# Index scores of a sparse-attention decoder step: cached keys as the moving operand, two units side by side

## Chip, cores and metric

One core of a Trainium2 chip runs the whole program. The metric is the device time of one execution, in microseconds (us); lower is better.

## The reference, cut to what matters

A two-layer decoder trunk is run once for a prompt of 1024 tokens and for 8 sample sequences of 8 tokens, each with 4096 cached positions. Layer 0 is sparse attention: an "indexer" with 4 heads of 64 dimensions scores every key for every query, and the 256 best are attended to. The change touches the index scores alone.

```python
# prompt: 1024 new tokens; sample: 8 sequences x 8 new tokens, each with 4096 cached positions
IDX_HEADS = 4
IDX_DIM = 64
IDX_SCALE = (IDX_DIM ** -0.5) * (IDX_HEADS ** -0.5)
...
def dsa_block(q, qi, wi, q_pos, k_all, v_all, ki_all, topk):
    L = k_all.shape[1]
    key_pos = jnp.arange(L, dtype=jnp.int32)
    logits = jnp.einsum('bqhd,bsd->bqhs', qi.astype(jnp.float32), ki_all.astype(jnp.float32))
    score = jnp.einsum('bqh,bqhs->bqs', wi.astype(jnp.float32), jax.nn.relu(logits)) * IDX_SCALE
    admissible = key_pos[None, :] <= q_pos[:, None]
    score = jnp.where(admissible[None], score, -jnp.inf)
    _, sel = lax.top_k(score, topk)
...
```

## The kernel before, in words

The program is a row of stages, each a block in which the engines run their own instruction lists and meet at a barrier at its end. `index_stage` computes the index projections; `score_stage` (lines 2848 to 3109) computes all index scores; `search_stage` begins after it and searches the 256th best score. TensorE (PE) is in order, and so is each other engine.

In `score_stage` two kinds of work share the engines.

**Units.** The cached index keys of the sample sequences are handled in 32 units: sequence b of 8 and quarter c of 4, each 1024 keys by 64 dimensions, held as 128 partitions by 512 values. GpSimd gathers them in groups of four (`IndexUnits.gather`, L2699, four indirect DMAs), with room for two groups: the gather of group k waits until unit 4k-5 has been turned (`turned`). `turn` (L2972) transposes a unit by four 128x128 transposes, ScalarE copies it to `kxT` (`key_copy`, L3026), and then four products of 64 columns (L3005) have the keys as the weights and the queries of the sequence (`q_pair`) as the moving operand. Each product is two fp32 passes, so a unit has eight weight loads of 128 columns. VectorE takes ReLU and the head weight in one instruction (`weigh`, L3086), and adds up the heads (`sum_heads`, L3094). The scores then lie with the keys on the partitions; `back` (L2981) transposes them once more, twice in a quarter, eight times in all, and ScalarE copies them with a stride to `Ss` (`back_copy`, L3034). The head weights reach all partitions by a product with ones (L2992).

**Works.** 44 `logit` works compute the new tokens' scores: s0 to s3 (64 columns) are the samples' new keys, then come four heads of each piece of the prompt's rows 2 to 7 (L2960, L2961; up to 512 columns). ScalarE takes ReLU (L3020), VectorE weighs and adds (L3075, L3078). The logits have two banks, so `logit(s)` waits for the ReLU of work s-2. Each of the units 0 to 11 has two works, each of the others one.

The stage's order on PE is: turn of unit i+1, works of unit i, products of unit i. GpSimd's list also holds the causal masks: two selects on the samples' new scores after work s3 (L2933, L2936) ahead of the gather of group 2, and one select for each prompt row block (L2946), placed by `masks_after` between the gathers; the one for row 2 waits for work s7 and stands ahead of gather 3, that for row 4 waits for s19 and stands ahead of gather 5.

Some products elsewhere in the program use a part of the array's columns: `sample_attention_stage` multiplies by weights of 32 columns, four products with four outputs of 32 partitions side by side, and keys of 512 columns as the moving operand (L3968).

Of the kernel before, what the change touches and what calls it, by code (L numbers as in the profile page):

```python
# [2847 lines left out]
def score_stage(nc, idx, wi_row, kidx_outs, units, room, Ss, Sp, prompt_level, g):  # L2848
# [7 lines left out]
    with Scope(nc, "sel") as S:  # L2856
        fresh = room.take(NS)[0:NS, :]
        by_key = room.take(NT * NB * NQ).rearrange("p (t b q) -> p t b q", t=NT, b=NB)
        ki_nat = room.take(NTT * ID).rearrange("p (n d) -> p n d", n=NTT)
        kxT = room.take(2 * 512).rearrange("p (s x) -> p s x", s=2)  # L2860
# [4 lines left out]
        weighed = room.low(TOK, 2 * UK * NQ * IH).rearrange("p (s t x) -> p s t x", s=2, t=UK)  # L2865
        w_all = room.low(TOK + 512, NS * IH).rearrange("p (b q h) -> p b q h", b=NB, q=NQ)
        w_row = room.low(TOK + 768, NS * IH)[0:IH, :].rearrange("p (b q h) -> p b q h", b=NB, q=NQ)
# [19 lines left out]
        backs_of = {i: [i // 8 * 2 - 2 + i % 8 - 2] if i >= 8 and i % 8 in (2, 3) else [] for i in range(len(units_))}  # L2887
        last_backs = range(2 * UNITS - 2, 2 * UNITS)
        turns = [("unit", 0)]
        for i in range(len(units_)):  # L2890
            if i + 1 < len(units_):
                turns.append(("unit", i + 1))
            turns += [("back", n) for n in backs_of[i]]
        turns += [("back", n) for n in last_backs]
        turn_no = {x: e for e, x in enumerate(turns)}
        assert len(turns) == len(units_) + NT // 4
# [4 lines left out]
        wb, small = S.ps("wb", [P, 512]), S.ps("small", [P, 512])  # L2901
        nat_of = lambda n: small[:, (n + 1) * ID:(n + 2) * ID] if n < 7 else wb[:, NS * IH + (n - 7) * ID:NS * IH + (n - 6) * ID]
        products, relu_ready, summed, masked = (S.sem(n) for n in ("products", "relu_ready", "summed", "masked"))
        q_zero, q_ready, w_row_ready, wb_ready, w_ready = (S.sem(n) for n in
                                                           ("q_zero", "q_ready", "w_row_ready", "wb_ready", "w_ready"))
        turned, kxT_ready, part_ready, part_used, by_key_ready = (S.sem(n) for n in ("turned", "kxT_ready", "part_ready",
                                                                                    "part_used", "by_key_ready"))
        back_turned, back_copied, begun = S.sem("back_turned"), S.sem("back_copied"), S.sem("begun")
# [4 lines left out]
        def wait_copied(eng, e):  # L2913

            kind, n = turns[e]
            eng.wait_ge(kxT_ready if kind == "unit" else back_copied, n + 1)

        @block.sync
        def _(sp):
            for n in range(NTT):  # L2920
                sp.wait_ge(i_copied, n + 1)
                sp.dma_start(i_p[n * P:n * P + rows(n), :] if n < NTT - 1 else i_s, ki_nat[0:rows(n), n, :]).then_inc(i_stored, 16)
            sp.wait_ge(i_stored, 16 * NTT)

        @block.gpsimd
        def _(pool):
            nc.gpsimd.memset(q_pair[:, :, :, :, :], 0.0).then_inc(q_zero, 1)
            nc.gpsimd.memset(Ss[0:NS, PAST // 2:], LOWEST).then_inc(begun, 1)
            nc.gpsimd.memset(prompt_level[:, :], 0.0)

# [19 lines left out]
        def _(pe):  # L2950
# [13 lines left out]
            def turn(i):  # L2964
                k, j = i // AHEAD, i % AHEAD
                if j == 0:
                    units.wait_loaded(pe, k)
                e = turn_no["unit", i]
                if e >= 2:
                    wait_copied(pe, e - 2)  # L2970
                for t in range(4):
                    last = nc.tensor.transpose(tr[e % 2][:, t * P:(t + 1) * P], kx[:, k % 2, j, t * P:(t + 1) * P],  # L2972
                                               g["ident"][:, :])
                last.then_inc(turned, 1)

            def back(n):
                e = turn_no["back", n]
                wait_copied(pe, e - 2)
                pe.wait_ge(by_key_ready, NB * (n // 2 + 1))
                for t in range(4):  # L2980
                    last = nc.tensor.transpose(tr[e % 2][0:NS, t * P:(t + 1) * P],  # L2981
                                               by_key[:, 4 * n + t, :, :].rearrange("p b q -> p (b q)"), g["ident"][:, :])
                last.then_inc(back_turned, 1)
# [10 lines left out]
            for i, (b, c) in enumerate(units_):  # L2994
                if i + 1 < len(units_):
                    turn(i + 1)
                for s in works_of[i]:
                    logit(s)
                if i == 0:
                    pe.wait_ge(q_ready, 2 * IH)  # L3000
                pe.wait_ge(kxT_ready, i + 1)
                if i >= 2:
                    pe.wait_ge(part_used, i - 1)
                for t in range(4):
# [3 lines left out]
                for n in backs_of[i]:  # L3008
                    back(n)
            for n in last_backs:  # L3010
                back(n)

        @block.scalar
        def _(act):
# [7 lines left out]
            def key_copy(i):  # L3022
                act.wait_ge(turned, i + 1)
                if i >= 2:
                    act.wait_ge(part_ready, i - 1)
                nc.scalar.activation(kxT[:, i % 2, :], tr[turn_no["unit", i] % 2][:, :], ACT.Copy).then_inc(kxT_ready, 1)  # L3026

            def back_copy(n):
                act.wait_ge(back_turned, n + 1)
                c, t0 = n // 2, 4 * (n % 2)  # L3030
                half, c = c // 2, c % 2

                dst = Ss[64 * half:64 * half + NS, c * 1024:(c + 1) * 1024].rearrange("q (p t) -> q t p", t=UK)
                nc.scalar.activation(dst[:, t0:t0 + 4, :],  # L3034
                                     tr[turn_no["back", n] % 2][0:NS, :].rearrange("q (t p) -> q t p", t=4),
                                     ACT.Copy).then_inc(back_copied, 1)

            key_copy(0)
            act.wait_ge(wb_ready, 1)
            nc.scalar.activation(w_all[:, :, :, :].rearrange("p b q h -> p (b q h)"), wb[:, 0:NS * IH], ACT.Copy,  # L3040
                                 scale=IDX_SCALE).then_inc(w_ready, 1)
            for i in range(len(units_)):
# [3 lines left out]
                if i + 1 < len(units_):  # L3046
                    key_copy(i + 1)
                for s in works_of[i]:
                    relus(s)
                for n in backs_of[i]:  # L3050
                    back_copy(n)
            for n in last_backs:
                back_copy(n)

        @block.vector
        def _(dve):
            for h in range(IH):
                nc.vector.tensor_scalar(w_row[:, :, :, h], wi_row[:, SEQ:TOK].rearrange("p (b q) -> p b q", b=NB),
                                        g["ident"][0:IH, h:h + 1], None, ALU.mult).then_inc(w_row_ready, 1)
# [21 lines left out]
            def weigh(i):  # L3081
                b, c = units_[i]
                dve.wait_ge(part_ready, i + 1)
                if i >= 2:
                    dve.wait_ge(by_key_ready, i - 1)
                nc.vector.scalar_tensor_tensor(  # L3086
                    out=weighed[:, i % 2, :, :], in0=part[i % 2][:, 0:UK * NQ * IH].rearrange("p (t x) -> p t x", t=UK),
                    scalar=0.0, in1=w_all[:, b, :, :].rearrange("p q h -> p (q h)").unsqueeze(1).to_broadcast([P, UK, NQ * IH]),
                    op0=ALU.max, op1=ALU.mult).then_inc(part_used, 1)

            def sum_heads(i):
                b, c = units_[i]
                dve.wait_ge(part_used, i + 1)
                nc.vector.tensor_reduce(out=by_key[:, UK * c:UK * (c + 1), b, :],  # L3094
                                        in_=weighed[:, i % 2, :, :].rearrange("p t (q h) -> p t q h", h=IH),
                                        axis=AX.X, op=ALU.add).then_inc(by_key_ready, 1)

            dve.wait_ge(wi_ready, 2)
            for i in range(len(units_)):
                for s in works_of[i]:  # L3100
                    add_head(s)
                if i == 0:
                    dve.wait_ge(w_ready, 1)
                if i < NTT:
                    nc.vector.tensor_copy(ki_nat[0:rows(i), i, :], nat_of(i)[0:rows(i), :]).then_inc(i_copied, 1)
                weigh(i)
# [1224 lines left out]
```

## Time and profile before

| | us |
|---|---|
| median of the 3 runs (2519.26 to 2523.59) | 2520.27 |
| profiled execution, its own time | 2533.14 |
| its span, first to last instruction | 2531.4 |
| PE busy over the span | 2444.0 (97%) |
| `score_stage`, first PE instruction to the last copy | 71.0 to 149.7 |

An engine that is busy for the whole span is not always the bound of each stage; the granted clock of PE (1.00 is 2.4 GHz, 0.50 is 1.2 GHz) changes what the same instructions take.

### The profile page before, as it was taken

Reading aid. Unit: us, or ns where it says so; the run is one execution under the profiler, and the core shown is the slowest. Engines: PE = TensorE matmul, PEld = TensorE weight load, DVE = VectorE, ACT = ScalarE, POOL = GpSimd, SP = SyncE. Lnnn points to the kernel's source line nnn. Section 1 sums busy time; section 2 is a strip of 40 time slices with the busy share of each in tenths; the row PEclk is TensorE's granted clock in tenths of the full one; section 3 lists DMA queues with packets and bytes.
Section 4 is the critical chain, followed back from the end, with each engine's and each line's share of the span. In section 5 each row is a group of like instructions: output and inputs, shape, how many; then the busy total and the mean of one; then the engine's idle time right before and its main releaser. Section 6 shows DMA issues by size and latency. Waiting matters only on the chain. (4 is left out here: it accounts for less than half of the span.)

```text
span 2531.4 us, 49311 instructions
## 1 busy us (share of the span) xinstructions
PE 2444.0 (97%) x18922; PEld 2332.5 (92%) x18953; DVE 1827.9 (72%) x3377; ACT 1130.0 (45%) x1928; POOL 108.3 (4%) x140
## 2 busy tenths in 40 slices
PE   8999898899999999999999999989999999999998
PEld 7899865577899999999999999989999999999998
DVE  6668867777558888886685686764798888768642
ACT  5567677686534433333222353553443434322221
POOL 1310132200000000000000000000000000000000
PEclk9899999999999999999999999999999999999999
DMA  6312499820022343433694423234143434449522
GB/s 213 88 51 80 145 332 361 329 84 1 21 100 70 139 147 138 147 138 124 241 321 150 134 73 113 68 94 168 56 139 138 148 138 151 140 177 351 193 91 84
DMA packets 279016, 371.91 MB, mean 147 GB/s; under 512 B 20747, under 2 KB 219651, under 8 KB 270662
## 3 DMA queue, kind: packets, MB, share of 16 engines
q1 hardware_dynamic: 266998, 294.23, 34.3%
q0 software_dynamic: 11776, 75.50, 8.1%
q8 instruction: 101, 1.65, 0.3%
q14 instruction: 61, 0.50, 0.1%
q10 hardware_dynamic: 80, 0.02, 0.0%
HBM read 271.07 MB, written 98.63 MB: 146 GB/s over the span
## 5 line engine op out<-in xcount | busy, mean ns | idle before, releaser
L1554 PE MATMUL ffn_acc<-trunk_x_ahead,trunk_w_hi 128*128 128x272 f32 x2464 | 466.5, 289 | 2.7 <-PEq L87 2.7
L1554 PE MATMUL ffn_acc<-ffn_x_later,ffn_w_hi_more 128*128 128x272 f32 x2112 | 397.1, 287 | 1.5 <-DVE trunk_xT L1203 1.4
L1554 PEld LDWEIGHTS ffn_acc<-trunk_x_ahead,trunk_w_hi 128*128 128x128 f32 x2464 | 385.3, 188 | 3.3 <-issue 3.3
L1554 PE MATMUL ffn_acc<-trunk_x_ahead,trunk_w_lo 128*128 128x272 f32 x1232 | 352.9, 286 | 0.0
L1554 PEld LDWEIGHTS ffn_acc<-ffn_x_later,ffn_w_hi_more 128*128 128x128 f32 x2112 | 330.9, 188 | 2.3 <-issue 2.3
L1554 PE MATMUL ffn_acc<-ffn_x_later,ffn_w_lo_more 128*128 128x272 f32 x1056 | 304.1, 288 | 0.0
L1554 PEld LDWEIGHTS ffn_acc<-trunk_x_ahead,trunk_w_lo 128*128 128x128 f32 x1232 | 232.5, 189 | 0.0
L1554 PEld LDWEIGHTS ffn_acc<-ffn_x_later,ffn_w_lo_more 128*128 128x128 f32 x1056 | 198.8, 188 | 0.0
L1445 DVE TENSOR_TENSOR trunk_xT<-ffn_acc,trunk_xT 128x544 f32<-128x544 f32 x168 | 121.4, 723 | 92.9 <-PE ffn_acc L1610 91.0
L1610 PE MATMUL ffn_acc<-trunk_x_ahead,trunk_w_hi 128*128 128x272 f32 x896 | 170.8, 289 | 0.0
L945 ACT ACTIVATE ffn_w_hi_more<-trunk_w_raw 128x512 fp32r<-128x512 f32 x132 | 83.3, 631 | 156.2 <-PE ffn_acc L1554 153.5
L945 ACT ACTIVATE trunk_w_hi<-ffn_w_sum 128x512 fp32r<-128x512 f32 x88 | 55.6, 632 | 210.2 <-DVE ffn_w_sum L1184 125.4
L1610 PE MATMUL ffn_acc<-ffn_x_later,ffn_w_hi_more 128*128 128x272 f32 x768 | 145.8, 287 | 0.1
L1634 PE MATMUL ffn_acc<-trunk_x_ahead,trunk_w_hi 128*128 128x364 f32 (+1 forms) x576 | 142.1, 328 | 0.0
L1610 PEld LDWEIGHTS ffn_acc<-trunk_x_ahead,trunk_w_hi 128*128 128x128 f32 x896 | 140.1, 188 | 0.4 <-issue 0.4
L1610 PE MATMUL ffn_acc<-trunk_x_ahead,trunk_w_lo 128*128 128x272 f32 x448 | 128.3, 286 | 0.0
L3321 PE MATMUL search_acc<-attxm_x_pairs,attxm_w_hi 128*128 128x364 f32 (+1 forms) x480 | 121.4, 334 | 1.9 <-PEq L87 1.9
L1610 PEld LDWEIGHTS ffn_acc<-ffn_x_later,ffn_w_hi_more 128*128 128x128 f32 x768 | 120.2, 188 | 0.7 <-issue 0.3
L1032 ACT ACTIVATE trunk_xT<-trunk_xT 128x544 fp32r<-128x544 f32 x112 | 71.7, 654 | 91.5 <-DVE trunk_xT L1264 48.8
L1610 PE MATMUL ffn_acc<-ffn_x_later,ffn_w_lo_more 128*128 128x272 f32 x384 | 110.5, 288 | 0.0
L1203 DVE TENSOR_TENSOR trunk_xT<-ffn_acc,ffn_u 128x544 f32<-128x544 f32 x88 | 63.5, 722 | 59.2 <-PE ffn_acc L1554 59.2
L1634 PEld LDWEIGHTS ffn_acc<-trunk_x_ahead,trunk_w_hi 128*128 128x128 f32 x576 | 101.8, 188 | 0.0
(523 smaller groups left out, 5994.6 us busy)
## 6 DMA issues: line engine op xcount, KB each, us to landing
o_kept<-trunk_xT SPq DMA_DIRECT2D x96, 544.0 KB, 4.4
trunk_w_raw<-in_ffn_w_gu SPq DMA_DIRECT2D x88, 512.0 KB, 4.0
trunk_x_ahead<-o_kept SPq DMA_DIRECT2D x56, 544.0 KB, 6.7
ffn_x_later<-o_kept SPq DMA_DIRECT2D x56, 544.0 KB, 7.3
x_saved<-trunk_xT SPq DMA_DIRECT2D x24, 544.0 KB, 2.7
trunk_xT<-x_saved SPq DMA_DIRECT2D x24, 544.0 KB, 6.6
o_kept<-trunk_xT SPq DMA_DIRECT2D x32, 272.0 KB, 4.9
trunk_w_raw<-in_sg_w_in SPq DMA_DIRECT2D x16, 512.0 KB, 4.0
```

Source lines behind the costliest of these rows:

```text
L945: nc.scalar.activation(w_parts(i)[0], source, ACT.Copy).then_inc(w_hi_ready, 1)
L1032: nc.scalar.activation(stage_hi[STAGE_OF[i][0]], raw_block[i], ACT.Copy).then_inc(kept_hi, 1)
L1203: nc.vector.tensor_tensor(two(out), pair(b), two(a), ALU.add).then_inc(done, 1)
L1445: nc.vector.tensor_tensor(two(out), pair(bank_of(z, n)), two(out), ALU.add).then_inc(d_added, 1)
L1554: last = nc.tensor.matmul(bank(2 * PAIR[p] + c)[:, 0:QC], w[:, k * P:(k + 1) * P], x(p, k)[:, c * QC:(c + 1) * QC], start=FRESH[p] and k = ...
L1610: last = nc.tensor.matmul(bank(2 * bank_of(z, n) + c)[:, 0:QC], w[:, k * P:(k + 1) * P], x(i, at)[:, c * QC:(c + 1) * QC], start=n in (0, ...
L1634: last = nc.tensor.matmul(bank(NC3 * (q % 2) + c)[:, 0:w], part[:, q % 2, k * P:(k + 1) * P], x[:, a:a + w], start=(k == 0 and j == 0), st ...
L3321: last = nc.tensor.matmul(banks[NC3 * (m % 2) + c][:, 0:w], part[:, k * P:(k + 1) * P], x_parts[x][:, k, a:a + w], start=(k == 0 and j == ...
```

## The change

The queries of a sequence (64 columns) are now the weights, and a unit's 512 transposed key columns are the moving operand. Two units are scored side by side: the even one has its output in partitions 0 to 63 of a bank, the odd one in 64 to 127. VectorE takes ReLU alone, over both units in one instruction (`gate`). The head weights and the scale stand in a masked matrix `w_sum`, built by nine GpSimd instructions and four on VectorE from weights that go through a small DRAM tensor; once in eight units (four pairs) eight products with weights of 32 columns (`sum_heads`) give the scores with the queries on the partitions. `back` and the product with ones are gone. VectorE (`left_out`) and ScalarE (`right_out`) copy the result to `Ss`, two strided copies each. Turns run two units ahead, with four buffers of `kxT` in place of two. The twelve extra works are spread over all 32 units: s3 is now in unit 2, s7 in unit 5, s11 in unit 8, s19 in unit 14. The order in which the keys' rows are stored is changed to 7, 8, 0 to 6. Gathers and masks keep their places and waits.

```diff
-        by_key = room.take(NT * NB * NQ).rearrange("p (t b q) -> p t b q", t=NT, b=NB)
-        kxT = room.take(2 * 512).rearrange("p (s x) -> p s x", s=2)
+        kxT = room.take(4 * 512).rearrange("p (s x) -> p s x", s=4)
+        first, second = room.low(TOK, 2 * 512), room.take(2 * 512)
+        gated = [v[:, 512 * i:512 * (i + 1)] for v in (first, second) for i in range(2)]
+        w_sum = room.take(4 * 2 * 4 * NQ).rearrange("p (m s b q) -> p m s b q", m=4, s=2, b=4)
+        w_cols = room.take(4)
...
-            n = 1 + (i < n_extra)
+            n = 1 + ((i + 1) * n_extra // len(units_) - i * n_extra // len(units_))
...
+            sp.dma_start(w_kept.rearrange("q h b -> h b q"), wi_row[:, SEQ:TOK].rearrange("h (b q) -> h b q", b=NB)
+                         ).then_inc(w_stored, 16)
+            sp.wait_ge(w_stored, 16)
+            for u in range(2):
+                for s in range(2):
+                    at = 64 * u + 32 * s
+                    sp.dma_start(w_cols[at:at + 32, :], w_kept.rearrange("q h (m u) -> u (q h) m", u=2)[u]).then_inc(w_loaded, 16)
...
+            nc.gpsimd.memset(w_sum[:, :, :, :, :], IDX_SCALE).then_inc(w_masked, 1)
+            pool.wait_ge(w_masked, 1)
+            for m in range(4):
+                v = w_sum[:, m, :, :, :]
+                nc.gpsimd.affine_select(out=v, in_=v, compare_op=ALU.is_ge, fill=0.0, base=128 * (m % 2),
+                                        pattern=[[-32, 2], [-64, 4], [-4, NQ]], channel_multiplier=1).then_inc(w_masked, 1)
...
+            def sum_heads(c):
+                pe.wait_ge(gated_ready, 4 * c + 4)
+                if c:
+                    pe.wait_ge(left_copied, 2 * c)
+                    pe.wait_ge(right_copied, 2 * c)
+                else:
+                    pe.wait_ge(w_ready, 4)
+                    pe.wait_ge(i_copied, NTT)
+                for odd in range(2):
+                    for quad in range(2):
+                        m = 2 * quad + odd
+                        for s in range(2):
+                            at = 64 * quad + 32 * s
+                            last = nc.tensor.matmul(sums_bank[quad][at:at + 32, :],
+                                                    w_sum[:, m, s, :, :].rearrange("p b q -> p (b q)"), gated[m],
+                                                    start=odd == 0, stop=odd == 1, skip_group_check=True)
+                last.then_inc(heads_summed, 1)
...
-            pe.wait_ge(w_row_ready, IH)
-            nc.tensor.matmul(wb[:, 0:NS * IH], g["ones"][0:IH, :], w_row[:, :, :, :].rearrange("p b q h -> p (b q h)"),
-                             start=True, stop=True).then_inc(wb_ready, 1)
...
-                for t in range(4):
-                    last = nc.tensor.matmul(part[i % 2][:, t * 64:(t + 1) * 64], kxT[:, i % 2, t * P:(t + 1) * P],
-                                            q_pair[:, b, :, :, :].rearrange("p s q h -> p (s q h)"), start=True, stop=True)
+            turn(1)
+            for j in range(n_pairs):
+                for i in (2 * j, 2 * j + 1):
+                    if i + 2 < len(units_):
+                        turn(i + 2)
+                    for s in works_of[i]:
+                        logit(s)
+                if j == 0:
+                    pe.wait_ge(q_ready, 2 * IH)
+                pe.wait_ge(kxT_ready, 2 * j + 2)
+                if j >= 2:
+                    pe.wait_ge(gated_ready, j - 1)
+                for u in range(2):
+                    i = 2 * j + u
+                    b, c = units_[i]
+                    last = nc.tensor.matmul(part[j % 2][64 * u:64 * (u + 1), :],
+                                            q_pair[:, b, :, :, :].rearrange("p s q h -> p (s q h)"), kxT[:, i % 4, :],
+                                            start=True, stop=True, skip_group_check=True)
                 last.then_inc(part_ready, 1)
+                if j and j % 4 == 0:
+                    sum_heads(j // 4 - 1)
+            sum_heads(n_pairs // 4 - 1)
...
+            def right_out(c):
+                act.wait_ge(heads_summed, c + 1)
+                for s in range(2):
+                    dst, src = sums_out(c, 1, s)
+                    nc.scalar.activation(dst, src, ACT.Copy).then_inc(right_copied, 1)
...
+            def gate(j):
+                dve.wait_ge(part_ready, j + 1)
+                if j >= 4:
+                    dve.wait_ge(heads_summed, j // 4)
+                nc.vector.tensor_scalar(gated[j % 4], part[j % 2][:, :], 0.0, None, ALU.max).then_inc(gated_ready, 1)
+
+            def left_out(c):
+                dve.wait_ge(heads_summed, c + 1)
+                for s in range(2):
+                    dst, src = sums_out(c, 0, s)
+                    nc.vector.tensor_copy(dst, src).then_inc(left_copied, 1)
```

## Rows read from the trace of the kernel before

**Rows 1.** The page: busy time, share of the span and instructions of each engine.
```profile
PE 2444.0 (97%) x18922; PEld 2332.5 (92%) x18953; DVE 1827.9 (72%) x3377; ACT 1130.0 (45%) x1928; POOL 108.3 (4%) x140
```
**Rows 2.** Stretches: length, then busy time of the five engines, clock, DMA share, GB/s.
```profile
71.00:149.70 78.70, 72.70 (x524) 68.05 (x524) 50.28 (x131) 45.58 (x86) 27.11 (x35) 0.89 0.31 85
71.20:84.85 13.65, 13.65 (x69) 12.49 (x67) 5.50 (x25) 4.42 (x11) 2.52 (x7) 0.50 0.03 7
84.85:125.80 40.95, 38.30 (x305) 35.90 (x305) 29.59 (x73) 26.71 (x52) 19.89 (x23) 1.00 0.50 134
122.40:125.80 3.40, 1.78 (x15) 1.68 (x15) 1.51 (x5) 2.80 (x5) 0.30 (x1) 1.00 0.31 93
125.80:129.20 3.40, 3.40 (x18) 3.40 (x18) 2.03 (x6) 1.09 (x2) 1.75 (x2) 0.50 0.14 19
```
**Rows 3.** Timeline of PE, three units: start, duration, engine, line, operation.
```profile
85.26 0.61 PE L2972 MATMUL sel_banks<-trunk_ident,att_proj 128*128 128x128 f32 x4
87.25 0.28 PE L2972 MATMUL sel_banks<-trunk_ident,att_proj 128*128 128x128 f32 x1
...
92.04 0.61 PE L2972 MATMUL sel_banks<-trunk_ident,att_proj 128*128 128x128 f32 x4
...
94.27 0.28 PE L2972 MATMUL sel_banks<-trunk_ident,att_proj 128*128 128x128 f32 x1
...
140.32 0.61 PE L2972 MATMUL sel_banks<-trunk_ident,att_proj 128*128 128x128 f32 x4
...
141.23 1.00 PE L3005 MATMUL sel_banks<-att_proj 128*128 128x64 f32 x8
142.07 0.28 PE L2972 MATMUL sel_banks<-trunk_ident,att_proj 128*128 128x128 f32 x1
```
**Rows 4.** Products with 32-column weights in the later stage: by line, then the timeline of PE.
```profile
L3968 PE MATMUL satt_sc<-satt_KT,satt_qs x256: 589/593/618, 320.7 to 474.0; 128*32 128x512 f32 x128
...
397.54 1.09 PE L3954 MATMUL satt_tr<-trunk_ident,cache_ring 128*128 128x128 f32 x8
398.78 1.07 PE L3968 MATMUL satt_sc<-satt_KT,satt_qs 128*32 128x512 f32 x8
399.77 0.33 PE L3954 MATMUL satt_tr<-trunk_ident,att_proj 128*128 128x128 f32 x1
```
**Rows 5.** Start of the stage, timeline of PE.
```profile
73.03 1.12 PE L2972 MATMUL sel_banks<-trunk_ident,att_proj 128*128 128x128 f32 x4
74.08 1.22 PE L2992 MATMUL sel_wb<-att_proj,trunk_ones 4*128 4x256 f32 x2
```
**Rows 6.** GpSimd ahead of gather 2, and stretches of 1 us around its landing.
```profile
81.36 0.28 POOL L2933 TENSOR_SCALAR_AFFINE_SELECT att_proj<-att_proj 64x64 f32<-64x64 f32 x1 [8.38 <-DVE att_proj L3078]
...
83.22 0.95 POOL L2699 DMA_INDIRECT att_proj<-in_cache_kidx,trunk_unit_row  x1 [1.16 <-PE sel_banks L2972]
...
90.00:91.00 1.00, 0.92 (x5) 0.62 (x5) 0.77 (x2) 1.00 (x4) 0.00 (x0) 1.00 0.16 45
91.00:92.00 1.00, 1.00 (x10) 0.96 (x9) 1.00 (x4) 1.00 (x3) 0.00 (x0) 1.00 0.00 0
```
**Rows 7.** Stalls inside the stage, of PE and of ScalarE.
```profile
108.19 0.66 PE L2972 MATMUL sel_banks<-trunk_ident,att_proj 128*128 128x128 f32 x4 [0.92 <-ACT scores_Ss L3034]
...
122.99 1.08 ACT L3034 ACTIVATE scores_Ss<-sel_banks 64x512 f32<-64x512 f32 x1 [2.20 <-remote]
...
124.12 0.66 PE L2972 MATMUL sel_banks<-trunk_ident,att_proj 128*128 128x128 f32 x4 [1.62 <-ACT scores_Ss L3034]
```
**Rows 8.** The end of the stage, timeline.
```profile
144.34 1.00 PE L3005 MATMUL sel_banks<-att_proj 128*128 128x64 f32 x8
...
147.06 1.03 PE L2981 MATMUL sel_banks<-trunk_ident,att_proj 128*64 128x128 f32 x8 [1.71 <-DVE att_proj L3094]
147.69 1.99 ACT L3034 ACTIVATE scores_Ss<-sel_banks 64x512 f32<-64x512 f32 x2 [2.55 <-PE sel_banks L2981]
```
**Rows 9.** Groups of VectorE by line and shape: busy us, mean ns, idle before.
```profile
L3086 DVE SCALAR_TENSOR_TENSOR att_proj<-sel_banks,att_proj 128x256 f32<-128x256 f32 x32 | 13.4, 418 | 3.8 <-PE sel_banks L3005 2.2 <-remote 1.6
...
L4147 DVE COPY satt_probT<-satt_tr 128x512 f32<-128x512 f32 x24 | 16.5, 686 | 5.0 <-PE satt_tr L4002 3.4 <-remote 1.3
```

More of the change, by code:

```diff
@@ L2885, in score_stage @@
         assert at_work == len(work) and 0 <= n_extra <= len(units_)
[L2887 to L2896, printed above, removed]
+        n_pairs = len(units_) // 2
+        keys_order = (7, 8) + tuple(range(7))
         banks = S.ps("banks", [P, 6 * 512])
@@ L2911, in score_stage, with sums_out @@
         block = S.block()
-        def wait_copied(eng, e):
-            kind, n = turns[e]
-            eng.wait_ge(kxT_ready if kind == "unit" else back_copied, n + 1)
+        def sums_out(c, quad, s):
+            rows, half = 64 * (c // 2) + 32 * quad, c % 2
+            dst = Ss[rows:rows + 32, half * 1024:(half + 1) * 1024].rearrange("q (p t s) -> q s t p", t=4, s=2)[:, s, :, :]
+            at = 64 * quad + 32 * s
+            return dst, sums_bank[quad][at:at + 32, :].rearrange("q (t p) -> q t p", t=4)
         @block.sync
         def _(sp):
-            for n in range(NTT):
-                sp.wait_ge(i_copied, n + 1)
+            sp.dma_start(w_kept.rearrange("q h b -> h b q"), wi_row[:, SEQ:TOK].rearrange("h (b q) -> h b q", b=NB)
[5 more added lines that the diff above has]
+                    sp.dma_start(w_cols[at:at + 32, :], w_kept.rearrange("q h (m u) -> u (q h) m", u=2)[u]).then_inc(w_loaded, 16)
+            for k, n in enumerate(keys_order):
+                sp.wait_ge(i_copied, k + 1)
                 sp.dma_start(i_p[n * P:n * P + rows(n), :] if n < NTT - 1 else i_s, ki_nat[0:rows(n), n, :]).then_inc(i_stored, 16)
@@ L2929, in _ @@
             nc.gpsimd.memset(prompt_level[:, :], 0.0)
+            nc.gpsimd.memset(w_sum[:, :, :, :, :], IDX_SCALE).then_inc(w_masked, 1)
[4 more added lines that the diff above has]
+                                        pattern=[[-32, 2], [-64, 4], [-4, NQ]], channel_multiplier=1).then_inc(w_masked, 1)
+            pool.wait_ge(w_masked, 5)
+            for m in range(4):
+                v = w_sum[:, m, :, :, :]
+                nc.gpsimd.affine_select(out=v, in_=v, compare_op=ALU.is_ge, fill=0.0, base=IH - 1 - 128 * (m % 2),
+                                        pattern=[[32, 2], [64, 4], [4, NQ]], channel_multiplier=-1).then_inc(w_masked, 1)
             pool.wait_ge(summed, IH)
@@ L3045, in _ @@
                     nc.scalar.activation(Ss[NS:P, PAST // 2:], fresh, ACT.Copy)
-                if i + 1 < len(units_):
-                    key_copy(i + 1)
+                if i + 2 < len(units_):
+                    key_copy(i + 2)
                 for s in works_of[i]:
                     relus(s)
[L3050 to L3053, printed above, removed]
+                if i > 8 and i % 8 == 2:
+                    right_out(i // 8 - 1)
+            right_out(UNITS - 1)
         @block.vector
         def _(dve):
-            for h in range(IH):
-                nc.vector.tensor_scalar(w_row[:, :, :, h], wi_row[:, SEQ:TOK].rearrange("p (b q) -> p b q", b=NB),
-                                        g["ident"][0:IH, h:h + 1], None, ALU.mult).then_inc(w_row_ready, 1)
             dve.wait_ge(nat_turned, NTT)
@@ L3101, in _ @@
                     add_head(s)
-                if i == 0:
-                    dve.wait_ge(w_ready, 1)
                 if i < NTT:
-                    nc.vector.tensor_copy(ki_nat[0:rows(i), i, :], nat_of(i)[0:rows(i), :]).then_inc(i_copied, 1)
-                weigh(i)
-                if i:
-                    sum_heads(i - 1)
-            sum_heads(len(units_) - 1)
+                    n = keys_order[i]
+                    nc.vector.tensor_copy(ki_nat[0:rows(n), n, :], nat_of(n)[0:rows(n), :]).then_inc(i_copied, 1)
+                if i == 4:
+                    dve.wait_ge(w_loaded, 16 * 4)
+                    dve.wait_ge(w_masked, 9)
+                    for m in range(4):
+                        nc.vector.tensor_scalar(w_sum[:, m, :, :, :], w_sum[:, m, :, :, :], w_cols[:, m:m + 1], None,
+                                                ALU.mult).then_inc(w_ready, 1)
+                if i % 2:
+                    gate(i // 2)
+                if i > 8 and i % 8 == 2:
+                    left_out(i // 8 - 1)
+            left_out(UNITS - 1)
 PIECE = TOK // 8
```

85 lines of the change are left out of this document (19 added, 66 removed).

## The prediction

> **What bounds the kernel now.** I read the page first: PE is busy for 97% of the span [rows 1], so PE's own list sets the time, stage by stage. The change lives in one stage, 71.0 to 149.7. Its stretches say that PE is busy for 72.7 of 78.7 us there, VectorE 50.3, ScalarE 45.6, and that the clock is not whole: it is 0.50 from 71.2 to 84.85 and again from 125.8 to 129.2 [rows 2]. So PE bounds this stage, and everything saved on PE counts once, unless PE then waits for something that is now hidden.
>
> The timeline of PE gives the cost of each piece. A unit with one 512-column work takes 142.07 - 140.32 = 1.75 us, one with two takes 94.27 - 92.04 = 2.23, one with two 384-column works 87.25 - 85.26 = 1.99 [rows 3]. So a 512-column work is 0.48, a 384-column one (1.99 - 1.27) / 2 = 0.36, and an empty unit 1.27. The products with the queries are 142.07 - 141.23 = 0.84 of that [rows 3] (0.83 below, so that the parts add up), the four transposes the other 0.44. Works narrower than 384 I take at 0.24, the nearest bound below being half of the 512's. All 44 works: 24 x 0.48 + 8 x 0.36 + 12 x 0.24 = 17.3 us. Before, at full clock, PE has 32 x 0.44 + 32 x 0.83 + 17.3 + 8 backs x 0.44 + 0.6 (half of the 1.2 that L2992 took at half clock [rows 5]) = 62.1 us. From 73.03 [rows 5] to 149.7 are 76.7. The other 14.6: the half clock gives away (84.85 - 73.03) / 2 = 5.9 and 1.7; PE's two stalls 1.6 and 0.9 [rows 7]; 3.4 at the end, where PE's list is dry but for a microsecond [rows 8]; 1.1 unassigned.
>
> **Scoring.** 32 x 0.83 = 26.6 goes. In its place are 16 pairs of two 64-column products with 512 moving columns, two fp32 passes each. The trace has no 64-column tile. Nearest are the 32-column ones: eight passes (four products) begin at 398.78 and the next PE work at 399.77, 0.99 us, while a single pass lasts 0.59 [rows 4]. Two rounds of four passes, 1.07 - 0.59 = 0.48 apart, fit; eight in a row don't. And 0.48 is what one pass costs alone: L2992, two passes of 256 columns at half clock, took 1.22 [rows 5], so some 0.5 for 512 at full. Between the transposes (eight by 0.11 from 397.54, over at 398.4) and 398.78 lie one bf16 product of 512 columns and a gap: about 0.1 for coming into this mode. So a pair costs 0.99 + 0.1 = 1.1, all of it on the path: 17.6 in all. Bounds: 0.95 (no gap) and, if two 64-column tiles don't overlap, 2.0.
>
> The Trainium skill bears on the gap (TensorEngine Tiling (Array Packing), Key Properties): changing the tiling mode drains the engine, and by its Restrictions fp32 transposes can't run in a column-tiled mode, so every pair pays twice. The rows agree with a small price. It also has a measured packing (TensorE: Matmul & The Clock Gate, Measured speedup vs the span model): three column tiles gave 2.38 times, not 3. By that ratio a pair would be some 0.2 dearer, 3 us in all, an estimate; the rows show four tiles at the cost of one.
>
> **Head sums.** Added: 4 x (8 products, 16 passes, four rounds). By the same rows 4 x 0.48 + 0.1 = 2.0, so 8.0. Removed: eight backs, 3.5, and L2992, 0.6 (1.2 as it ran). Bounds: 1.8, or 7 each if nothing overlaps.
>
> **PE's list after:** 14.1 + 17.3 + 17.6 + 8.0 = 57.0 against 62.1: 5.1 us less.
>
> **Other engines.** VectorE loses 32 x (0.42 + 0.41) and gets 16 gates; a copy of 128x512 from PSUM takes 0.69 [rows 9]; so it falls by 15 us, less 8 strided copies of 0.7 to 1.1 and four small scalings. ScalarE has eight strided copies as before (1.0 to 1.1 each [rows 8]). Per pair ScalarE then has some 4.75 instructions of 0.5 and a quarter of 2.2, 2.9 us, against PE's 3.6; it doesn't become the bound. SyncE's round trip through DRAM (5 small DMAs, ahead of the key rows) has over 10 us until VectorE wants `w_cols` in unit 4; GpSimd's nine new instructions of 0.3 lie in the idle 8.4 us ahead of 81.36 [rows 6]. Both cost nothing; without the cover, 2 to 3 us. The spread of the works moves no PE time by itself.
>
> **What comes late next: gathers.** The gather of group 2 stands behind the selects that wait for s3. At half clock PE does turns 0 to 2, s0, turn 3, s1, pair 0 (about 2.0) and turn 4 by 80.3, s2 and s3 by 81.15; before, s3's last pass began at 79.94 and the selects at 81.36 [rows 6]. So the selects start near 82.4 and the gather near 83.2, as before (83.22). Its traffic ended in the slice 90 to 91 [rows 6]: landed near 90.3, 7.1 us after. But PE now comes to `turn(8)` in unit 6, not 7, and with less behind it: 8 turns, s0 to s7 and three pairs, 3.5 + 2.4 + 3.3 = 9.2 us of full-clock work, 5.9 of it done by 84.85, so at 88.2. It waits 2.2 us for the gather. A wait like that had a price before: in 122.4 to 125.8 PE was busy for 1.78 of 3.40 and the next 3.4 us ran at 0.50 [rows 2]. I take the same here: 1.7 more.
>
> From 90.4 the rest is 57.0 - 9.2 - 2.0 = 45.8, with the 1.7 to 137.9. Gather 5 waits in GpSimd's list for s19, now in unit 14: PE is there near 107.3, ReLU, sum and select bring it to 108.9, landing 116.0; `turn(20)` is due at 114.7. Another 1.3: the last scores are done at 139.2. Gathers 3, 4, 6 and 7 come out 0.7 us or more ahead of their turns.
>
> **The end.** From the last score: gate 0.7 and latencies 0.2, sums 2.0, two strided copies one behind the other 2.1, about 5.2, against 149.68 - 145.34 = 4.3 before [rows 8]. Stage end: 144.4 against 149.7, 5.3 us less. The stalls of ScalarE and VectorE that come from elsewhere ("remote", 2.2 us [rows 7]) cost before 2.5 and a clock step; turns two units ahead hide part. I charge 1.5 for what is left. That makes **3.8 us less**. Against the profiled execution: span 2531.4 - 3.8 = 2527.6, its own time 2533.1 - 3.8 = 2529.3; the runs shown are 12.9 below it in the median, so 2520.3 - 3.8 = 2516.5. The search stage behind moves as a block.
>
> **Rivals.**
> - *The gathers don't bite* (the selects come earlier, or the clock doesn't fall): no 2.2, no 1.3, no 1.7, less of the 1.5: 8 to 9 us less, 2512. For it: gathers 3 to 7 are in time even by my sums. Against it: gather 2 by 2 us. 0.20.
> - *Two 64-column tiles take turns* in place of overlapping: 16 x 0.88 = 14.1 more, and the waits for gathers (5.2 with the clock) vanish: 14.1 - 5.2 - 3.8 = 5 more than before, 2525. It decides from 0.25 us per pair on. Against it: four tiles overlap [rows 4]; for it: no row has this width. 0.07.
> - *More half clock*: each wait at a gather or a stall costs 1.7 on top, and two more of them leave no gain, 2520. Also the case that the whole change is swallowed. For it: one stall of 1.6 did it before [rows 2, 7]. 0.13.
> - *The overlap is partial*: a pair costs 1.3, between the bounds 1.1 and 2.0. 16 x 0.2 = 3.2 of the gain go: 2519.7. Against it: four tiles went in the time of one [rows 4]. 0.05. The packing ratio of the Trainium skill named above would give just this case.
>
> The forecast keeps 0.55. A measurement of this kernel tells about 0.2% (5.0 us) from no change. The forecast's own range, 2514 to 2519, has a third beyond that line; with the first rival that makes faster 0.38, slower (over 2525.3) 0.06, and 0.56 within. Range 2510.5 to 2522: it takes in the first and third rival and leaves out the tiles that take turns.
>
> **What the profile after would show.** Right: the four passes of a pair of units starting in twos, 0.45 to 0.5 apart; PE idle at `turn(8)` with the gather of group 2 as releaser; half clock after it; score stage ending near 145 to 146. Wrong: passes starting one by one (second rival); no DMA among PE's waits and an end near 141 (first); waits of PE on `kxT` or `gated` that I hold for hidden.

## The result, and the profile after

The kernel before ran in 2522.02 us (median of 20 runs), the changed one in 2527.40 (20 runs): a ratio of 1.0021, 95% interval 1.0014 to 1.0027. It is 5.4 us slower where 3.8 us less was forecast, and the time lies outside the range of 2510.5 to 2522.

The page of the changed kernel; PE's share is a point lower than in [rows 1].

```profile
PE 2434.4 (96%) x18760; PEld 2300.2 (91%) x18791; DVE 1825.6 (72%) x3337; ACT 1129.7 (45%) x1927; POOL 110.0 (4%) x149
```

Stretches of the score stage after, with the columns of [rows 2]: the whole stage to the first product of the next, the three stretches at half clock, the end.

```profile
71.34:150.49 79.15, 65.64 (x362) 36.64 (x363) 47.87 (x91) 45.35 (x85) 28.87 (x44) 0.91 0.31 84
72.35:75.76 3.41, 3.41 (x20) 3.00 (x18) 2.43 (x10) 1.20 (x2) 2.97 (x12) 0.50 0.07 3
...
86.00:92.83 6.83, 4.17 (x14) 3.31 (x14) 0.62 (x2) 2.27 (x4) 3.94 (x5) 0.50 0.76 206
...
116.72:120.14 3.42, 3.17 (x14) 2.95 (x14) 1.01 (x3) 2.00 (x4) 2.07 (x3) 0.50 0.78 228
...
144.66:150.18 5.52, 1.92 (x16) 0.42 (x16) 3.43 (x4) 2.15 (x2) 0.29 (x1) 1.00 0.00 0
```

PE is busy for 65.6 us of a stage of 79.2, against 72.7 of 78.7 [rows 2]: seven microseconds less of busy time, and no less time in all. The clock is whole again at 75.76, nine microseconds earlier than before, and falls twice later.

The timeline of PE after: start, duration, operation, and in brackets the idle time ahead of it and who ended it.

```profile
72.81 2.92 PE L2984 MATMUL sel_banks<-trunk_ident,att_proj 128*128 128x128 f32 x12
...
76.52 1.08 PE L3027 MATMUL sel_banks<-att_proj 128*64 128x512 f32 x4
77.53 0.65 PE L2984 MATMUL sel_banks<-trunk_ident,att_proj 128*128 128x128 f32 x4
...
80.67 0.66 PE L2984 MATMUL sel_banks<-trunk_ident,att_proj 128*128 128x128 f32 x4
81.08 0.42 PE L2973 MATMUL sel_banks<-idx_k_hi,idx_q 128*128 128x384 f32 x1
...
81.51 0.60 PE L2984 MATMUL sel_banks<-trunk_ident,att_proj 128*128 128x128 f32 x4
81.87 0.43 PE L2973 MATMUL sel_banks<-idx_k_hi,idx_q 128*128 128x384 f32 x1
...
82.94 1.08 PE L3027 MATMUL sel_banks<-att_proj 128*64 128x512 f32 x4
88.66 1.11 PE L2984 MATMUL sel_banks<-trunk_ident,att_proj 128*128 128x128 f32 x4 [4.64 <-DMA att_proj<-in_cache_kidx,trunk_unit_row]
...
104.06 0.66 PE L2984 MATMUL sel_banks<-trunk_ident,att_proj 128*128 128x128 f32 x4 [0.88 <-ACT att_proj L3048]
...
109.77 0.66 PE L2984 MATMUL sel_banks<-trunk_ident,att_proj 128*128 128x128 f32 x4
110.18 0.48 PE L2973 MATMUL sel_banks<-idx_k_hi,idx_q 128*128 128x512 f32 x1
110.50 0.40 PE L2974 MATMUL sel_banks<-idx_k_lo,idx_q 128*128 128x512 f32 x1
110.73 0.60 PE L2984 MATMUL sel_banks<-trunk_ident,att_proj 128*128 128x128 f32 x4
...
111.41 0.40 PE L2974 MATMUL sel_banks<-idx_k_lo,idx_q 128*128 128x512 f32 x1
111.74 1.08 PE L3027 MATMUL sel_banks<-att_proj 128*64 128x512 f32 x4
112.75 0.62 PE L3001 MATMUL sel_left<-att_proj 128*32 128x512 f32 x2
...
116.97 1.11 PE L2984 MATMUL sel_banks<-trunk_ident,att_proj 128*128 128x128 f32 x4 [2.30 <-DMA att_proj<-in_cache_kidx,trunk_unit_row]
```

The passes of the scoring by themselves, from the table by line and shape (count, then busy us and mean ns of one):

```profile
L3027 PE MATMUL sel_banks<-att_proj 128*64 128x512 f32 x64 | 17.3, 618 | 0.0
```

The scoring of a pair (L3027) takes 77.53 - 76.52 = 1.01; 64 passes of 618 ns cover 17.3 us and not 39.6, so they overlap. From 111.41 to 111.74 lie 0.33 where 0.23 lie between the same product and a transposition (110.50 to 110.73): 0.10 for coming into the mode in which several outputs lie side by side. A pair costs 1.11. Coming out costs 0.05 more: four transpositions take 81.08 - 80.67 = 0.41 behind a pair, 81.87 - 81.51 = 0.36 behind another product. The eight head-sum products that begin at 112.75 are over at 116.97 - 2.30 = 114.67, 1.92 later. At 82.94 + 1.01 = 83.95 PE wants the keys of group 2 and waits 4.64 us.

GpSimd after, ahead of gathers 2 and 5 (four instructions each, the first shown), and the waits of PE in the stage: us in total, times, longest.

```profile
79.89 0.28 POOL L2946 TENSOR_SCALAR_AFFINE_SELECT att_proj<-att_proj 64x64 f32<-64x64 f32 x1 [4.12 <-DVE att_proj L3090]
...
81.00 0.95 POOL L2699 DMA_INDIRECT att_proj<-in_cache_kidx,trunk_unit_row  x1 [0.41 <-issue]
...
108.57 0.29 POOL L2959 TENSOR_SCALAR_AFFINE_SELECT masks_Sp<-masks_Sp 128x128 f32<-128x128 f32 x1 [6.34 <-DVE masks_Sp L3090]
109.25 1.11 POOL L2699 DMA_INDIRECT att_proj<-in_cache_kidx,trunk_unit_row  x1 [0.38 <-issue]
```

```profile
PE sel_banks L2984 <- DMA att_proj<-in_cache_kidx,trunk_unit_row: 6.9, 2, 4.6
...
PE sel_banks L2984 <- ACT att_proj L3048: 1.8, 3, 0.9
```

The selects begin at 79.89, 1.5 earlier than in [rows 6], and the gather's keys are there 88.66 - 81.00 = 7.7 us after its first instruction. PE, which I had forecast at this turn for 88.2, has been there since 83.95. Gather 5 stands behind a select (108.57) in the same manner.

The end of the stage after, and two of VectorE's groups.

```profile
143.58 1.08 PE L3027 MATMUL sel_banks<-att_proj 128*64 128x512 f32 x4
...
145.27 0.68 DVE L3097 TENSOR_SCALAR att_proj<-sel_banks 128x512 f32<-128x512 f32 x1
...
146.01 0.62 PE L3001 MATMUL sel_left<-att_proj 128*32 128x512 f32 x2 [1.36 <-DVE att_proj L3097]
...
148.00 2.16 DVE L3103 COPY scores_Ss<-sel_left 32x512 f32<-32x512 f32 x2 [2.05 <-PE sel_small L3001]
148.00 2.18 ACT L3054 ACTIVATE scores_Ss<-sel_small 32x512 f32<-32x512 f32 x2 [3.67 <-PE sel_small L3001]
```

```profile
L3097 DVE TENSOR_SCALAR att_proj<-sel_banks 128x512 f32<-128x512 f32 x16 | 11.0, 685 | 4.7 <-PE sel_small L3001 4.7
L3103 DVE COPY scores_Ss<-sel_left 32x512 f32<-32x512 f32 x8 | 8.7, 1089 | 2.2 <-PE sel_small L3001 2.0
```

From the end of the last scores (143.58 + 1.08) to the end of the copies (150.18) are 5.5 us, against 4.3 before [rows 8].

### The profile page after: what moved, and what is told of

Same layout as the page of the kernel before. It is cut to its first block and busy times, and to the rows that moved or that the text cites. A ratio compares the mean times of both kernels' runs of the same rounds, so it can differ in the third digit from the quotient of the medians.

```text
span 2529.8 us, 48922 instructions
## 1 busy us (share of the span) xinstructions
PE 2434.4 (96%) x18760; PEld 2300.2 (91%) x18791; DVE 1825.6 (72%) x3337; ACT 1129.7 (45%) x1927; POOL 110.0 (4%) x149
```

## Experiments

The theory after the result: PE's work did shrink, and the two gathers give it back. The rivals: the spread of the works costs by itself; the strided copies of ScalarE do; the loss lies in a later stage. Ratios are against the kernel before on the same chip (medians 2527.45, 2522.97 and 2527.28 on the three occasions). A ratio is taken over the runs, not from the two medians, and differs from their quotient by up to 0.0007.

**The changed kernel, works as before.** `n = 1 + (i < n_extra)` in place of the spread; all else changed.

> The changed kernel with one part undone: units 0 to 11 carry two works each again, as before the change. Theory 1 (the spread puts works s3, s7 and s19 later, GpSimd's selects wait for them in front of the gathers, PE waits at turn 8 and turn 20 and then runs at half clock): the 4.6 us and 2.3 us waits shrink to under 2 us in sum, and the kernel is 3 to 6 us faster than the changed one, ratio to the kernel before 0.999 to 1.001. Rival 2 (the column-tiled products or the long end of the stage cost it): no change against the changed kernel, ratio near 1.002. Rival 3 (the loss lies in a later stage): also near 1.002, with the score stage no shorter.

2525.45 us, 0.9989 (0.9980 to 0.9998), just below the ratio expected. PE's wait for gather 2 is 1.30 us at 87.12, none is left for gather 5. ScalarE holds PE up by 1.08 and 1.08 for its ReLUs and later by 0.94, 2.26 and 0.67 for key copies. The 0.94 and the 2.26 come just behind 5.40 us in which ScalarE stood idle:

```profile
115.91 0.60 ACT L3048 ACTIVATE att_proj<-sel_banks 128x512 f32<-128x512 f32 x1 [5.40 <-remote]
```

The profile names nothing in the program that ended this wait ("remote"); its cause is open, and none of the four profiles of the changed kernel has one like it. The stage is 75.0 us long. With two works in every early unit PE comes later to the same turn, so the spread carries part of the loss; that it does so only through the gathers is tested further below.

**The changed kernel, gathers first.** Gather 2 ahead of the selects, all prompt masks behind the last gather.

```diff
+            pool.wait_ge(turned, AHEAD)
+            units.gather(pool, 2)
             pool.wait_ge(summed, IH)
...
-            masks_after = {2: [2], 3: [3], 4: [4], 5: [], 6: [5], 7: [6, 7]}
+            masks_after = {2: [], 3: [], 4: [], 5: [], 6: [], 7: [2, 3, 4, 5, 6, 7]}
             for k in range(2, len(units_) // AHEAD):
-                pool.wait_ge(turned, AHEAD * (k - 1))
-                units.gather(pool, k)
+                if k > 2:
+                    pool.wait_ge(turned, AHEAD * (k - 1))
+                    units.gather(pool, k)
```

> The changed kernel, its spread kept, but GpSimd issues the gather of group 2 ahead of the selects on the new samples' scores, and all six masks on the prompt's rows come after the last gather. Theory 1: PE no longer waits for a gather by more than 1 us, the drops to half clock at 86 to 93 and 117 to 120 go, the stage is 7 to 11 us shorter than in the changed kernel: ratio to the kernel before 0.997 to 0.9995. Rival 2 or 3: ratio 1.001 to 1.003, waits gone but the time where it was.

2521.66 us, 0.9973 (0.9964 to 0.9982). GpSimd's timeline, the stage's stretch, and PE's waits behind ScalarE in this kernel:

```profile
77.01 0.95 POOL L2699 DMA_INDIRECT att_proj<-in_cache_kidx,trunk_unit_row  x1 [0.92 <-PE sel_banks L2987]
```

```profile
71.65:143.52 71.87, 62.66 (x363) 33.83 (x363) 47.65 (x91) 45.04 (x85) 29.57 (x44) 0.98 0.33 93
```

```profile
100.19 0.66 PE L2987 MATMUL sel_banks<-trunk_ident,att_proj 128*128 128x128 f32 x4 [1.17 <-ACT att_proj L3051]
...
115.53 0.66 PE L2987 MATMUL sel_banks<-trunk_ident,att_proj 128*128 128x128 f32 x4 [0.84 <-ACT att_proj L3051]
```

The gather starts 4.0 us earlier than at 81.00, no wait for a gather is left, and the clock is at half only for 3.4 us near the start: the stage is 71.9 long. A second set of runs:

> The changed kernel with all gathers first again, beside the one with only the gather of group 2 first, and to be set against the split copies: ratio to the kernel before 0.9973 to 0.9990. If the split of the strided copies is worth 1.5 to 2.5 us, this is 0.0006 to 0.001 above 0.9982.

2522.37 us, 0.9980 (0.9971 to 0.9990), stage 71.0. The sign of the result turns with the order of GpSimd's list.

**The kernel before with the works spread** (the one line).

> The kernel before with the spread of the works alone. Theory 1: the gather of group 2 comes some 3 us later and that of group 5 some 2 us later; PE turns one unit ahead and has more to do in front of turn 8, so only the wait at turn 20 opens: 0 to 3 us slower, ratio 1.000 to 1.0012. Rival 2: no difference to the kernel before. If the spread alone cost 5 us, the rest of the change would be worth nothing.

2529.89 us, 1.0009 (0.9999 to 1.0018): no wait for a gather, so that expectation missed; but in its one profile the half clock at the start lasted longer, and the stage is 80.7 us long.

```profile
70.86:91.34 20.48, 20.48 (x93) 19.48 (x91) 8.82 (x31) 7.36 (x17) 5.00 (x9) 0.50 0.20 60
```

PE was busy for all of these 20.48 us. The ratio of the spread alone, some 2 us, can't be told from none.

**Both edits in the changed kernel.**

> The changed kernel with both edits: two works in each of units 0 to 11, and the gathers ahead of all selects. Theory 1: the same as with the gathers first alone, within 1.5 us, since the spread costs only through GpSimd's list: ratio 0.997 to 0.9995. If ScalarE or VectorE were the bound in units with two works, this would be slower than the one with the spread kept by more than 2 us.

2521.99 us, 0.9983 (0.9974 to 0.9992), stage 73.8. With the gathers early, the spread no longer costs: with the works as before the kernel is not faster than with gathers first alone. Its profile again has a "remote" wait of ScalarE, of 5.41 us, with a wait of PE of 2.25 behind it.

**The changed kernel again**, to see the scatter.

> The changed kernel itself once more, beside the next three on one chip, so that they are compared with it directly. All theories: the ratio to the kernel before is 1.000 to 1.003. Its profile shows again a wait of PE for the gather of group 2 of 3 to 5 us and one of 1 to 3 us at group 5, whatever the stage's phase against the clock.

2527.60 us, 1.0023 (1.0014 to 1.0032): waits for gathers of 4.55 and 2.30, stage 78.3.

**The kernel before with gathers first.**

> The kernel before with only GpSimd's order changed, gathers ahead of the selects. Its PE never waited for a gather. Theory 1: no change, ratio 0.9992 to 1.0008, so the gain of the same edit in the changed kernel (ratio 0.9973 on another chip) belongs to the new scoring once its gathers are in time. Rival: the early gathers help by themselves (they keep clear of other engines' instruction fetches, say); then this ratio is also near 0.998.

2522.48 us, 1.0002 (0.9993 to 1.0011), stage 73.7. Early gathers alone bring nothing to the time, so what they bring to the changed kernel is its own loss undone.

**Gathers first, strided copies split.** In both lists one copy at a time:

```diff
-                if i > 8 and i % 8 == 2:
-                    right_out(i // 8 - 1)
+                if i > 8 and i % 8 in (2, 5):
+                    right_out(i // 8 - 1, [i % 8 // 5])
```

> The changed kernel with gathers first, and the two strided copies of each quarter's sums on ScalarE and VectorE set apart: one after the works of unit 2, the other after those of unit 5 of the next eight. In the profile with gathers first PE waited 1.17, 0.84 and 0.64 us for ScalarE's key copies behind those two copies. Theory: these waits shrink to under 0.3 each, 1.5 to 2.5 us less than with gathers first: ratio to the kernel before 0.995 to 0.9975. Rival: ScalarE is behind for another reason (a late instruction fetch), then the waits stay and the ratio is as with gathers first.

2517.11 us, 0.9982 (0.9972 to 0.9993), above the 0.995 to 0.9975 expected. The stage is down to 68.3 and the waits at 100.19 and 115.53 above are gone; a small one for gather 2 appears.

```profile
71.43:139.69 68.26, 62.04 (x363) 33.74 (x363) 48.13 (x91) 44.90 (x85) 29.88 (x44) 0.97 0.36 97
```

```profile
84.54 0.66 PE L2987 MATMUL sel_banks<-trunk_ident,att_proj 128*128 128x128 f32 x4 [0.44 <-DMA att_proj<-in_cache_kidx,trunk_unit_row]
```

PE is 1.4 us earlier at this turn than with gathers first (84.10 against 85.54), because that profile has a wait of 1.21 us for a ReLU of ScalarE at 83.98, ahead of all strided copies, and this one doesn't. So not all of the 3.6 us between the two stages is the split's. The ratio is not better than that of gathers first (0.9973 and 0.9980): the trace shows the waits removed, the times can't tell it.

**The same, with no works in the last two units** (`n = (i + 1) * len(work) // 30 - i * len(work) // 30 if i < 30 else 0`).

> As the one before, and the 44 works spread over units 0 to 29 so that the last pair has none. Theory on the stage's end: VectorE has no three heads left to add when the last pair is scored, the last gate starts at once and the end of the stage, 5.5 us from the last score to the last copy in the changed kernel, shrinks by 0.5 to 0.8 us; ratio within 0.0006 of the one before. The last quarter's sums and strided copies, some 4 us, stay.

2515.47 us, 0.9977 (0.9968 to 0.9986), 7.5 us below before by the medians, 5.8 by the ratio, which overlaps with those of the split copies and of gathers first. The stage is 68.1 long. The end did not get shorter, against what was expected (6.7 us from the last scores to the last copy, 5.5 in the changed kernel): VectorE now has a strided copy between the last two gates, and PE waits longer ahead of the last sums (1.36 in the changed kernel, at 146.01 above).

```profile
134.10 0.62 PE L3004 MATMUL sel_left<-att_proj 128*32 128x512 f32 x2 [2.50 <-DVE att_proj L3100]
```

**Gather 2 first, the masks where they were.**

> The changed kernel with one edit: the gather of group 2 goes ahead of the selects on the new samples' scores; all other masks and gathers keep their order. Theory 1: the 4.6 us wait at turn 8 and the two half-clock stretches behind it go, the 2.3 us wait at turn 20 stays: 5 to 8 us less than the changed kernel, ratio to the kernel before 0.9985 to 1.000; the rest of the gain of the version with all gathers first belongs to group 5. If the clock were not tied to the wait, the stretch of half clock near 86 to 92 would stay.

2526.38 us, 0.9994 (0.9985 to 1.0003). The wait at turn(8) is gone, and with it the half clock that stood there; a wait for gather 3 is new, the one for gather 5 stays:

```profile
95.50 0.66 PE L2987 MATMUL sel_banks<-trunk_ident,att_proj 128*128 128x128 f32 x4 [1.46 <-DMA att_proj<-in_cache_kidx,trunk_unit_row]
...
114.18 0.65 PE L2987 MATMUL sel_banks<-trunk_ident,att_proj 128*128 128x128 f32 x4 [2.42 <-DMA att_proj<-in_cache_kidx,trunk_unit_row]
```

Gather 2 holds the larger part of the loss (1.0022, the mean of 1.0021 and 1.0023, to 0.9994), the masks ahead of later gathers the rest (to 0.9976, the mean of 0.9973 and 0.9980). In this profile the clock was at half for 6.8 us at the start, not 3.4.

**Single executions of both kernels**, each with its own profile, to see what is typical of the stage. What stood open ahead of the last two of each kernel was whether the loss lies in this stage or in a later one.

> The kernel before, a look at its profile. The profile of before on which the prediction rests had a 1.6 us and a 0.9 us stall of PE behind ScalarE and a stretch of half clock after the first, 4.2 us in all; the version of before with gathers first had none of them (score stage 73.7 us against 79.0) and yet the time of before. Theory: they are an accident of that one execution: here the score stage takes 73 to 76 us. Rival: they belong to this kernel, and the other order of GpSimd's list removed them: 78 to 80 us again.

> The same kernel, a second look, since one execution alone misled: by the theory 73 to 76 us in the score stage unless one of the stalls shows up again; by the rival 78 to 80.

> The kernel before again, for one look: a score stage of 76 to 79 us, with one stretch of half clock of 13.65 us at its start and stalls of 0.8 to 1.6 us behind ScalarE. Theory: the mean of the looks is 2 us or more below the changed kernel's. Rival: within 1 us of it.

> As before_look3: 76 to 79 us for the score stage; a mean of the looks near 77 or less by the theory.

> The changed kernel again, for one look. If the loss sits in the score stage (theory), this stage is 78 to 80 us long, against 76 to 79 before, with waits of PE for gather 2 (4.5 us) and gather 5 (2.3) and half clock after both. If it sits later (rival), the stage is near 77.4, before's mean, and the search, sample attention or state-space stages are longer than in the looks at before by 3 to 4 us together.

> As after_look1: 78 to 80 us for the score stage by the theory, near 77.4 by the rival.

The times were 2524.44, 2528.48, 2523.09 and 2518.75 for the kernel before, 2523.08 and 2526.03 for the changed one. Lengths from the profiles, from the first PE instruction of the stage to the first of the next one, in us:

| | score stage | mean | sample attention stage |
|---|---|---|---|
| before | 79.0 (the profile shown), 76.2, 77.0, 73.7, 73.8 | 75.9 | 175.8 to 185.1 |
| after | 79.2 (the profile shown), 78.3, 78.2, 79.8 | 78.9 | 175.3 to 180.7 |

Spans less these two stages average 2268.5 us in both groups. The single executions of before mostly missed the ranges expected for them: the first two lie between the theory's 73 to 76 and the rival's 78 to 80, the second with one of the stalls back, as its expectation allowed; the last two lie below 76 to 79. Those of after are in theirs, and the means are 3.0 us apart, where 2 or more was the sign that the loss lies in this stage. Below are the waits of PE inside the stage in the first and the second single execution of before, behind ScalarE's copy of scores; the whole stage of the third and its only marked wait, at the end; and the first single execution of after, with its two stretches at half clock:

```profile
105.03 0.66 PE L2972 MATMUL sel_banks<-trunk_ident,att_proj 128*128 128x128 f32 x4 [0.80 <-ACT scores_Ss L3034]
...
120.18 0.66 PE L2972 MATMUL sel_banks<-trunk_ident,att_proj 128*128 128x128 f32 x4 [0.86 <-ACT scores_Ss L3034]
```

```profile
123.75 0.66 PE L2972 MATMUL sel_banks<-trunk_ident,att_proj 128*128 128x128 f32 x4 [1.56 <-ACT scores_Ss L3034]
```

```profile
70.53:144.27 73.74, 70.12 (x524) 66.46 (x525) 50.07 (x131) 45.40 (x86) 26.85 (x35) 0.90 0.32 91
71.42:85.07 13.65, 13.65 (x64) 12.50 (x63) 5.83 (x23) 4.42 (x11) 3.40 (x8) 0.50 0.10 25
```

```profile
141.33 1.03 PE L2981 MATMUL sel_banks<-trunk_ident,att_proj 128*64 128x128 f32 x8 [1.71 <-DVE att_proj L3094]
```

```profile
70.56:148.79 78.23, 64.28 (x362) 35.29 (x363) 47.59 (x91) 45.25 (x85) 28.88 (x44) 0.93 0.31 85
71.40:74.82 3.42, 3.42 (x22) 3.02 (x20) 2.33 (x10) 1.19 (x2) 2.81 (x12) 0.50 0.10 7
...
85.06:91.88 6.82, 4.03 (x14) 3.32 (x14) 0.62 (x2) 2.11 (x4) 4.09 (x5) 0.50 0.74 207
```

These are executions of the same two programs. At its cleanest the stage of before is 73.7 us: the stalls of [rows 7] and the half clock at 125.8 [rows 2] are absent. Three of the five profiles of before have such stalls, two have none. All four of after lie above 78, with waits for gathers of 4.55 to 4.64 and 2.2 to 2.5 us in each. The third of before and the first of after, set against each other, balance: PE's idle time goes from 73.74 - 70.12 = 3.6 to 78.23 - 64.28 = 13.9, 10.3 more; its busy time at half clock from 13.65 to 3.42 + 4.03 = 7.45, which gives back half the difference, 3.1; and what is left, the work itself, falls by 10.3 - 3.1 - (78.23 - 73.74) = 2.7.

## Why the prediction was wrong, point by point

- **Scoring, right.** 1.1 per pair forecast, 1.01 and 0.10 measured, and 0.05 behind it that the sum had not. Two 64-column products of 512 overlap fully; the rival in which they take turns and the one of partial overlap (1.3 per pair) are out. Entering the mode costs what the rows of the 32-column tiles had shown.
- **Head sums, right.** 2.0 forecast, 1.92 measured. In an undisturbed stretch two units with a 512-column work each now take 112.75 - 109.77 = 2.98 us, against 2 x 1.75 before [rows 3]: 16 x 0.52 = 8.3 saved, 4.1 of backs and L2992 besides, 4 x 1.9 = 7.6 added: 4.8 less, by these prices, against 5.1 forecast.
- **"PE's list after: 5.1 us less", too much.** Over the whole stage the list shrinks by 2.7, not 4.8. Part is in the waits themselves: the instruction ahead of one runs to its end alone, where otherwise the next would overlap it. The third single execution of before has one such gap in PE's time, the first of after has eleven; by the single records this comes to about 1.3 of the 2.1, an estimate. The rest was not settled.
- **"What comes late next: gathers": the mechanism right, the size wrong. This is the step that failed, and what made the kernel slower than before.** Forecast were waits of 2.2 and 1.3, and 1.7 for the clock behind them, 5.2 in all. Measured were waits of 4.6 and 2.3; undoing them (gathers first) makes the stage 7.4 us shorter (78.9 against 71.9 and 71.0) and takes the ratio from 1.0021 and 1.0023 to 0.9973 and 0.9980, which is 11.5 us; the same edit does nothing to the time of the kernel before (1.0002). The wait at `turn(8)` was sized too small because I held the clock at half until 84.85, as in [rows 2]. It rose at 75.76, so PE stood at `turn(8)` at 83.95, not 88.2, while the selects, the four instructions of the gather and its landing moved far less (88.66 against 90.4). The earlier clock bought little by itself: PE ran faster into a wait whose end GpSimd sets, and the clock fell again at 86.00, in the middle of it.
- **The reference, wrong.** I counted the gain against 78.7 us of one profile. That execution held 2.5 us of stalls behind ScalarE, where two of the five have none, and 3.4 us at half clock in mid-stage [rows 2], where the other four have none; the five average 75.9. I charged 1.5 of such stalls to the changed kernel, whose four profiles have none that "remote" ends, and subtracted the gain from a median of runs that mostly, by these profiles, had not paid the full price.
- **ScalarE, "doesn't become the bound", right in the mean and wrong in the place.** Its eight strided copies come in twos and hold a key copy back: PE waits of 0.88 (104.06), and waits for ScalarE of 3.1 us in all in the first single execution of after, where 1.5 was charged for another cause. With the copies split no marked wait for a key copy is left.
- **The end:** 5.2 forecast, 5.5 measured. A strided copy is 1.09, from the upper end of the bounds.
- **Rival "more half clock":** in the profile after the clock does fall at each of the two gather waits, in two others of its four only at the first. The total at half is 3.41 + 6.83 + 3.42 = 13.7 us, as much as before has at its start alone, and 10.2 in those two others. More half clock is not what made it slower; the waits are.
- **The sum.** The stage forecast at 74.9 us (to the end of the copies, 0.3 ahead of the next product) is 78.6: 3.7 more. Before was taken 3.1 too long. 3.7 + 3.1 = 6.8 of the 9.2 us between forecast and result. Of the 3.7, the gathers are 2.2 (7.4 against 5.2); the rest is PE's list and ScalarE. So by lengths of the stage the reference is the largest single item. By times the gathers are: undoing them gives 11.5 us where 5.2 were charged, and the kernel without them is 5.9 us faster than before where 9.0 would follow from the forecast; but each of these figures is uncertain by some 2 us. The remaining 2.4 are not found in any stage: the profiles of before differ by 9 us in the sample attention stage alone, and the rest of the span is equal. Whether the change reaches that stage through the clock stays open.

## What to carry to other kernels

When PE's list shrinks, work out its arrival at each transfer with the clock at its highest, not as the trace of before had it: that is the case in which the wait is longest. An early order of gathers cost nothing here and decided over the sign of the change. And read several profiles of before ahead of subtracting from one: a stage that differs by 5 us between executions can't serve as the reference for a gain of 5.

## What the runs showed of the hardware

- Two fp32 products with 64-column weights and 512 moving columns, with their outputs in partitions 0 to 63 and 64 to 127, overlap fully: 1.01 us for the four passes, which last 0.62 each, with 0.10 more for coming into the mode and 0.05 for the transpositions behind it. Eight products with 32-column weights, sixteen passes, took 1.92.
- The granted clock at the start of the stage was 0.50 for 13.65 us in all five profiles of before, for 20.48 in the kernel before with the works spread, and for 3.4 in all four profiles of the changed kernel (6.8 in its variant with gather 2 first), though PE was busy for the whole of each stretch. It had risen at 75.76, ahead of the first 512-column scoring product at 76.52; behind twelve transpositions in a row, where before has the small product L2992 and the 64-column scoring products. What of this lifted it was not taken apart.
- A copy of 32 partitions by 512 values out of PSUM with a strided target took 1.09 us on VectorE, more than an instruction over 128 partitions by 512 in a row (0.69).
- Four indirect DMA instructions of a gather begin 1.25 us apart, and the keys are there 7.7 us after the first.
